# The D-skip term of a Mamba-2 scan: from a VectorE product to diagonal matmuls in the PSUM accumulation

## The reference, cut to what matters

```
h = rmsnorm(x);  proj = h @ w_in          # z_ssd, x/B/C, dt, q, k, v, z_sb, gates
xs, B, C = silu(conv4(xbc));  dt = softplus(dt_raw + dt_bias);  a = -exp(a_log)
# scan, per chunk and head:
attn   = (C B^T) * exp(segment sums of dt*a), lower triangle
y_diag = attn @ (xs * dt)
y_off  = exp(cumsum) * (C @ prev_state);  prev_state = decay * prev_state + B^T (xs*dt*decay)
y      = y_diag + y_off + xs * d_skip[head]          # the D-skip term is the last product
y      = group_rmsnorm(y * silu(z_ssd)) @ w_ssd_proj
o      = stick_breaking(q, k, v) * silu(z_sb) @ w_sb_proj
out    = x + rmsnorm((sigmoid(g1) * y_ssd + sigmoid(g2) * y_sb) @ w_out)
```

## Time and profile before

| | |
|---|---|
| runs | 1963.42 us median of 3 (1962.96 to 1964.13) |
| profiled execution | 1959.76 us; span 1958.1 us on its slowest core (core 4) |
| spans of the 8 cores | 1953.8 to 1958.1 us |
| TensorE | busy 1495.8 us (76%) |
| ScalarE | busy 1210.3 us (62%) |
| VectorE | busy 912.4 us (47%) |

### The profile page before, as it was taken

One profiled execution on the slowest core, in us unless ns is written; L12 is line 12 of the kernel. 1 busy time (PEld: TensorE's weight loads), 2 busy tenths in 40 slices (PEclk: granted clock), 3 DMA queues, 4 the chain that ended last, 5 costly groups with the idle time before them and its releaser, 6 DMA issues.

```text
span 1958.1 us, 28450 instructions; the slowest of 8 cores (1953.8 to 1958.1 us)
## 1 busy us (share of the span) xinstructions
PE 1495.8 (76%) x7452; PEld 722.4 (37%) x7452; DVE 912.4 (47%) x1822; ACT 1210.3 (62%) x2508; POOL 52.2 (3%) x58
## 2 busy tenths in 40 slices
PE   1666456666666988877988789877777789999984
PEld 1333254444443534422343234432222234444431
DVE  4455537888887553433443344433333322323344
ACT  2355414445445088999899988999999952221132
POOL 0000000000000300000000000000000010000000
PEclk9988757777777999999999999999999999999997
DMA  7710020000000111000010000110000071242056
GB/s 191 114 23 1 0 33 1 1 1 1 1 1 1 22 12 23 3 10 1 1 23 12 1 1 2 22 23 1 1 1 1 1 95 14 22 42 24 11 162 194
DMA packets 52186, 53.48 MB, mean 27 GB/s; under 512 B 19648, under 2 KB 45376, under 8 KB 52032
## 3 DMA queue, kind: packets, MB, share of 16 engines
q0 software_dynamic: 43824, 24.38, 10.8%
q1 hardware_dynamic: 8208, 27.27, 4.5%
HBM read 67.64 MB, written 8.39 MB: 39 GB/s over the span
## 4 chain that ended last, share of the span: by engine, by line
PE 44%; ACT 25%; DVE 14%; issue 12%; DMA 4%; ACTq 0%; DVEq 0%; SPq 0%; POOLq 0%
PE ps L384 15%; ACT et L824 7%; ACT wtb L854 6%; ACT spb L830 6%; PE ps L864 5%; DVE acc L455 4%; PE ps L390 4%; PE ps L583 3%; PE ps L952 3%; PE ps L957 3%; PE ps L847 3%; DMA y<-xb 3%; PE ps L817 2%; PE ps L851 2%; DVE Lmat L564 2%
## 5 line engine op out<-in xcount | busy, mean ns | idle before, releaser
L824 ACT ACTIVATE et<-ps 128x512 f32<-128x512 f32 (+3 forms) x640 | 375.5, 587 | 89.5 <-PE ps L821 63.9
L830 ACT ACTIVATE spb<-et 128x512 bf16<-128x512 f32 (+3 forms) x640 | 401.1, 627 | 1.6 <-ACT wtb L854 0.4
L384 PE MATMUL ps<-hT,wst 128*128 128x512 bf16 x1664 | 389.4, 390 | 6.2 <-issue 3.0
L838 DVE TENSOR_TENSOR Ssum<-Ssum,spb 128x512 bf16<-128x512 bf16 (+3 forms) x512 | 193.2, 377 | 415.9 <-ACT spb L830 325.9
L854 ACT ACTIVATE wtb<-ps 128x512 bf16<-128x512 f32 (+3 forms) x640 | 381.4, 596 | 2.6 <-PE ps L851 2.3
L864 PE MATMUL ps<-wtb,vtok 128*128 128x512 bf16 (+3 forms) x640 | 220.5, 344 | 155.5 <-ACT wtb L854 149.6
L384 PEld LDWEIGHTS ps<-hT,wst 128*128 128x128 bf16 x1664 | 164.9, 100 | 203.8 <-issue 28.0
L847 PE MATMUL ps<-spb,cb 128*128 128x512 bf16 (+3 forms) x640 | 220.9, 345 | 10.2 <-ACT spb L830 4.3
L817 PE MATMUL ps<-qz,kT 128*128 128x512 bf16 (+3 forms) x640 | 220.3, 346 | 0.0
L851 PE MATMUL ps<-Ssum,cb 128*128 128x512 bf16 (+3 forms) x576 | 197.1, 342 | 0.0
L864 PEld LDWEIGHTS ps<-wtb,vtok 128*128 128x128 bf16 x640 | 61.5, 96 | 337.7 <-issue 329.2
(11 more groups left out here) (111 smaller groups left out, 1613.8 us busy)
## 6 DMA issues: line engine op xcount, KB each, us to landing
xbuf<-x SPq DMA_DIRECT2D x17, 512.0 KB, 3.6
xb<-x SPq DMA_DIRECT2D x16, 512.0 KB, 4.4
y<-xb SPq DMA_DIRECT2D x16, 512.0 KB, 5.1
wst<-w_in POOLq DMA_DIRECT2D x12, 512.0 KB, 9.7
wst<-w_in POOLq DMA_DIRECT2D x5, 1024.0 KB, 12.5
wst<-w_in POOLq DMA_DIRECT2D x16, 256.0 KB, 6.2
wz<-w_in POOLq DMA_DIRECT2D x2, 1024.0 KB, 15.7
wA<-w_ssd_proj POOLq DMA_DIRECT2D x2, 1024.0 KB, 17.3
```

The costliest lines, as they stand in the source:

```text
L384: K.op("pe", lambda e, c=c: e.matmul(ps[bank][:], lhsT=wt[:, c, coff:coff + 128], rhs=hT[:, c, g * 512:(g + 1) * 512], start=(c == 0), sto ...
L824: K.op("act", lambda e: e.activation(out=e_[:, q0:512], in_=ps[bA][:, q0:512], func=AF.Exp), r=[B_ps[bA]], w=[be])
L830: K.op("act", lambda e: e.activation(out=s__[:, q0:512], in_=e_[:, q0:512], func=AF.Ln, bias=1.0, scale=1.0), r=[be], w=[bsp])
L838: K.op("dve", lambda e: e.tensor_tensor(out=Sn[:, q0p:512], in0=So[:, q0p:512], in1=s__[:, q0p:512], op=ALU.add), r=[bSo, bsp], w=[bSn])
```

## The change

The D-skip product L596 and its `yield` go. Ahead of the scan's loop VectorE builds 32 diagonal 128x128 bf16 matrices `DI`: for each head D rounded to bf16, and the remainder of D, again on a diagonal. In `front`, each of the 16 matmuls of L618 is followed by two more of the same shape, with the two diagonal matrices of its head as stationary operand and the same slice of `xs_tok` as moving operand, accumulated into the same 64 columns. The two additions of L623 become plain copies from PSUM. In the lines of the changed kernel everything behind L553 stands 14 lines further down at first, 13 after the shortened loop: L583 is L597, L609 is L618, L618 is L628 with the new L632, L623 is L637, L638 is L651, L658 is L671, L676 is L689, L688 is L701.

```diff
--- before.py
+++ after.py
@@ -553,6 +553,20 @@
     B_prev = [Buf(), Buf()]
     prevbf = sb("prevbf", [128, 1024], BF16)
     B_prevbf = [Buf(), Buf()]
+    DI = sb("DI", [128, 32, 128], BF16)
+    B_DI = Buf()
+    dsp = sb("dsp", [128, 48])
+    dspb = sb("dspb", [128, 16], BF16)
+    B_dsp = Buf()
+    K.op("dve", lambda e: e.tensor_copy(out=dspb[:], in_=hv[:, 32:48]), r=[B_par], w=[B_dsp])
+    K.op("dve", lambda e: e.tensor_copy(out=dsp[:, 0:16], in_=dspb[:]), r=[B_dsp], w=[B_dsp])
+    K.op("dve", lambda e: e.tensor_tensor(out=dsp[:, 16:32], in0=hv[:, 32:48], in1=dsp[:, 0:16], op=ALU.subtract),
+         r=[B_dsp, B_par], w=[B_dsp])
+    for h in range(16):
+        for k_ in range(2):
+            K.op("dve", lambda e, h=h, k_=k_: e.tensor_scalar(out=DI[:, 2 * h + k_, :], in0=CF(CI_ID),
+                                                               scalar1=dsp[:, 16 * k_ + h:16 * k_ + h + 1], scalar2=None, op0=ALU.mult),
+                 r=[B_dsp, B_cf], w=[B_DI])
     sst = sb("sst", [128, 8])
     B_sst = [Buf(), Buf()]
     B_sst2 = Buf()
@@ -593,11 +607,6 @@
             in1=dts[:, 6, c, :].unsqueeze(2).to_broadcast([128, 16, 64]), op=ALU.mult),
             r=[B_xs[c], B_dts], w=[bxw])
         yield
-        K.op("dve", lambda e: e.tensor_tensor(
-            out=yA_[:].rearrange("p (h d) -> p h d", h=16), in0=xs_tok[:, c, :].rearrange("p (h d) -> p h d", h=16),
-            in1=hv[:, 32:48].unsqueeze(2).to_broadcast([128, 16, 64]), op=ALU.mult),
-            r=[B_xs[c], B_par], w=byA)
-        yield
         for r_ in range(4):
             if r_ + 1 < 4:
                 seg(r_ + 1)
@@ -615,14 +624,18 @@
             for hh in range(4):
                 h = r_ * 4 + hh
                 g = h // 8
-                K.op("pe", lambda e, h=h, g=g: e.matmul(
-                    ps[5 + g][:, (h % 8) * 64:(h % 8 + 1) * 64], lhsT=attnT[:, h, :], rhs=xs_tok[:, c, h * 64:(h + 1) * 64],
-                    start=True, stop=True), r=[B_attn[h], B_xs[c]], w=[B_ps[5 + g]])
+                osl = ps[5 + g][:, (h % 8) * 64:(h % 8 + 1) * 64]
+                K.op("pe", lambda e, h=h, osl=osl: e.matmul(
+                    osl, lhsT=attnT[:, h, :], rhs=xs_tok[:, c, h * 64:(h + 1) * 64],
+                    start=True, stop=False, skip_group_check=True), r=[B_attn[h], B_xs[c]], w=[B_ps[5 + g]])
+                for k_ in range(2):
+                    K.op("pe", lambda e, h=h, osl=osl, k_=k_: e.matmul(
+                        osl, lhsT=DI[:, 2 * h + k_, :], rhs=xs_tok[:, c, h * 64:(h + 1) * 64],
+                        start=False, stop=(k_ == 1), skip_group_check=True), r=[B_DI, B_xs[c]], w=[B_ps[5 + g]])
             yield
         for g in range(2):
-            K.op("dve", lambda e, g=g: e.tensor_tensor(out=yA_[:, g * 512:(g + 1) * 512], in0=ps[5 + g][:],
-                                                       in1=yA_[:, g * 512:(g + 1) * 512], op=ALU.add),
-                 r=[B_ps[5 + g], byA[g]], w=[byA[g]])
+            K.op("dve", lambda e, g=g: e.tensor_copy(out=yA_[:, g * 512:(g + 1) * 512], in_=ps[5 + g][:]),
+                 r=[B_ps[5 + g]], w=[byA[g]])
             yield
 
     def back(c):
```

## The result

| | median, us | ratio to before (95%) |
|---|---|---|
| before | 1963.6 | |
| changed kernel | 2007.7 | 1.022 (1.0209 to 1.0232) |

The changed kernel is 44 us slower. The sum gave +31.9, the forecast 1995; the measured time is near the upper end of the range (1978 to 2011). In some executions of every kernel the cores of one die, or of both, run longer at a lower granted clock; the ratios and the spans of executions given here leave those out.

The account below looks back on a forecast made before the run. It took the chain of z projection, SiLUs, table load and Exp into `dec` to bound the loop, not VectorE. Loop 18.2 + setup 11.7 + first chunk 2 = +31.9 us on the median 1963.4 gave 1995.3; range 1978 to 2011.

Parts of the forecast that it names:

- the projection queued behind block 0: Loop, TensorE: z projection L390 now stands behind block 0, starts 2.5 us later per iteration, delaying the third group's `dec`.
- The bound: VectorE's wait for the third group's `dec` ends by projection, SiLUs, table load, Exp; removing L596's 1.13 us ahead gains nothing.
- VectorE's 83%: VectorE's busy share of the 14 full iterations; sole support for the 4% rival that VectorE paces the loop, 1947 us.
- the slack: Between the projection's end and the second SiLU: 0.8 us per iteration, taken off the projection's 2.5 us delay.
- the sum: Per iteration: +2.5 - 0.8 + 0.05 - 0.45 = +1.3 us, bounds +0.9 and +1.8; times 14, +18.2 us.
- The diagonal matmuls: TensorE, block 1 behind the projection: 12 matmuls, each with a weight load of 0.097, take 1.1 us.
- The clock credit: Transposes and L635 at iteration's end run at clock 1.00 through denser TensorE work: -0.45 us per iteration, bounds 0 and 0.8.
- The rival: TensorE's wait in block 0 makes its clock rise later, slowing the projection: +1.8 us x14, 25 us more, 2020 us; 10%.
- a projection at half speed: Listed sign of being wrong: the loop's z projection running at TensorE's lower clock; an earlier one took 5.43 against 3.62 us.
- Ahead of the loop: 35 VectorE instructions building the diagonal matrices before the first `Lmat`, 32 at 0.34 us: +11.7 us, bounds 6 and 15.
- First chunk and iteration 0: `front(0)` and iteration 0: extra weight loads in four blocks between `seg`s on TensorE cost +2 us, bounds 0 and 4.
- the sum of all upper bounds: Loop 25, setup 15, first chunk and iteration 0 4: +44 us, that is 2007 us.

Follow-up runs that it names:

- matrices built in the wait: Changed kernel with the diagonal matrices built before VectorE's wait for `exa`: 1993.7 us; with the empty yield put back too: 1969.2 us.
- the run without L596: Kernel before with L596 left out, its yield kept, additions from PSUM made copies, D-skip term missing from the result: 1962.1 us, 1.0008.
- the run with the yield: Changed kernel with one empty yield put back where L596 stood, restoring the order of the kernel before: 1982.9 us, 1.0104.
- The moved projection: Changed kernel, matrices built before the wait for `exa`, z projection moved from `back(c)` into `front(c)`: 1933.3 us, 0.9856.
- filling the gap: Changed kernel with four idle 128x256 matmuls in block 0 behind the second head, where TensorE waits for VectorE: 2000.9 us, 1.0196.
- the fastest order: z projection moved into `front(c)`, yield between L591 and L596 gone: 1933.3 us with the fold, 1936.6 with L596 instead, 1932.9 without diagonal matmuls.

## Why the prediction was right, and where its sum was short

The sign and the main mechanism, the projection queued behind block 0, held; the loop was to take about 321 us and took 331.7. The steps from the kernel before to the changed one, each between two kernels that differ in it alone: L596 away, +0.2 us (not distinguishable from 0); diagonal matmuls, with their matrices built in the wait, +7.2; matrices built ahead of the loop instead, +13.7 (1982.9 less 1969.2); order, +24.8 (2007.7 less 1982.9). These four are one path, so they give 46 us by construction, the 44 measured and the 2 by which the kernel before differed between groups. What checks them is the second price of the matrices, in the other order: +14.0 (2007.7 less 1993.7).

*The bound.* "In such a wait a VectorE instruction removed ahead of it is worth nothing" is what the run without L596 showed for the time, and VectorE's 83% was no bound. The reason given was only half right. In the iteration of the rows the SiLUs did not wait for the projection (timeline of ScalarE, kernel before):

```profile
418.16 0.63 ACT L660 ACTIVATE prevbf<-prev 128x512 bf16<-128x512 f32 x1 [1.41 <-DVE prev L658]
418.79 1.28 ACT L665 ACT_TABLE_LOAD   x1
```

Their table load stood right behind the copy L660, which waited for VectorE's second L658, and that one stood behind L596. So VectorE, and L596 with it, was a link of the chain in 10 of the 14 iterations; in the 4 with a slow projection the load waited for L390. Without L596 the load comes up to 0.9 us earlier, waits for the projection in all 14 iterations, and the next load then waits 0.55 us for `seg(2)` in all 14. The wait for `dec` grew by 7 us, not by L596's 17. That a second chain, over TensorE, stood so close behind the first that nothing was left of the gain I had not read from the rows; this part came out by luck.

*The projection behind block 0.* Start predicted at 418.5 - 409.0 = 9.5 us into the iteration; it was 9.4. VectorE's third group was predicted at 15.9; it was 16.1 (469.45 less 453.36). The missing 0.2 is a step that I had not seen: with the projection later, `seg(2)` ends after the SiLUs, and the table load ahead of Exp waits for it too, 0.35 us. From the third group to the second L688 (now L701) 5.2 us were predicted and 5.17 measured (469.45 to 474.62). One reading in the working is slightly off: half way through the pair of SiLUs is 420.62, not 420.55, which makes the slack 0.9 and the sum 0.1 smaller.

*The diagonal matmuls.* I put a block of 12 at 1.1 us, from 12 weight loads of 0.097. When its products are ready, a block takes 0.35 us (in the run with the yield it starts at 410.74, and `seg(2)` behind it at 411.09): the loads overlap, and their duration is not their spacing. Of the 5.8 us that they cost in the loop in the order of before, 3.2 come from where they stand, between projection and `seg(2)`: the table load ahead of Exp waits 0.78 us in each of 14 iterations with them, 0.55 without. Another 1.2 us are slower projections (6 over 4 us, where the run without L596 has 4); the rest is not taken apart. In the new order block 0 stands ahead of the projection and is mostly covered by the wait for VectorE.

*The clock credit, the step that failed.* I took off 0.45 us per iteration because denser work would hold TensorE's clock up to the transposes. It did not: they and L648 ran at 0.50 as before. The work was not dense up to block 3, which fits the price above: a head's three matmuls take 0.09 us and not 0.29, while VectorE delivers a head every 0.26, so TensorE stands idle between heads (windows, from block 2 on):

```profile
469.90:473.30 3.40, 2.09 (x24) 1.37 (x24) 3.40 (x10) 1.86 (x6) 0.00 (x0) 0.79 0.00 0
```

The moved projection did bring what the credit was for: there L655 took 0.38. Without the credit the sum gives +1.75; the undisturbed iteration grew by 2.0 (21.27 in the one of the rows, 23.27 now), and slow projections did the rest. I had them as a rival with 10% and 25 us. The rival was real in size per case (1.4 to 1.6 us over 3.61) and happened in 4 of 14 iterations here, 6 us; it is also the one sign of being wrong that came ("a projection at half speed"). But the kernel before has slow projections as well, without that wait ahead of them: 4 of its 14 took 4.2 to 4.5 us and one 3.8, 3 us in all. So on the cores profiled the change adds about 3 us by them, and filling the gap, which got 6.8 us back, removed more than the change had added. "TensorE: Matmul & The Clock Gate" of the Trainium skill, "Why this matters for your kernels", asks for TensorE to be kept busy without long gaps, and by that the added matmuls were to help. The trace does not bear this out for the matmuls of the change, and does for the four of the filled gap.

*Ahead of the loop.* Predicted 11.7, measured 13.1 in the trace: 0.39 per instruction and not 0.34. The gap between linked instructions was right (0.10 against 0.11); the duration was 0.286, what the trace had for 256 elements, not the 0.23 that I drew between 16 and 256. By what the Trainium skill says in "VectorE: DVE Perf Modes", "The DRAIN you can't avoid", that the semaphore costs nothing extra, there would be no gap; the trace disagrees for instructions that wait for the one before, with 3.5 us of idle time ahead of 32.

*First chunk and iteration 0.* Predicted +2, measured -0.2, where the cores of the kernel before differ by 1.3 us among themselves. That blocks are cheap, as above, would explain it; no run took it apart.

So of the 12 us by which the median missed the forecast, the loop's share is the largest: 28.8 against 18.2, of which 6.3 are the credit that was not paid and about 3 the slow projections. The loop and the setup together missed by 12.0 us, and the 2.2 that the first chunk did not cost hid a part of it. The measured 2007.7 lies just above 2007, the sum of all upper bounds; it is in the range because that was drawn "somewhat over the upper bound".

## What to carry to other kernels

Before you take work off the busiest engine, look at what ends its waits, and at what stands close behind that: here chains over TensorE and ScalarE held the loop, and 18 us of VectorE work could be deleted without effect. When the program's order comes from generators that are interleaved by `yield`, removing an instruction together with its step reorders all engines; print the order of both and look for a long instruction group that slid behind a dependency. Build constants ahead of a wait, not behind it (14 us here). Move the long independent piece (the z projection) out of the chain first, and try it in more than one order: the move alone gave 5 us in the order of before and 27 in the other, with the fold or without.

## What the runs showed of the hardware

- TensorE's granted clock rises at a time within the iteration that differs from iteration to iteration, though the work is the same: 6.0 to 8.8 us into ten iterations of the changed kernel and 12.3 to 12.7 into four, whose projections took 5.04 to 5.25 us instead of 3.61. A wait of 0.95 us or more for VectorE stands ahead of fast and slow projections alike. With four matmuls in that wait none of 14 was slow, on any core. Two more for comparison: the kernel before, without that wait, had 4 of 14 at 4.2 to 4.5 us, and the one with the yield alone taken out had 12 of 14 at 4.9 to 5.3.
- Small matmuls 128x64 with a fresh 128x128 bf16 weight load each come 0.03 us apart at the higher clock when nothing is waited for (12 in 0.35 us), though the record of a load lasts 0.1 us.
- A VectorE tensor_scalar from f32 to bf16 took 0.286 us for 128x128, as much as one from f32 to f32 for 128x256 (0.29). They differ in the output type and in the scalar, which the first reads from a tile and the second has as a constant; no run took this apart.
- A ScalarE table load of 1.28 us was not hidden in the wait of the instruction behind it: in the row at 464.73 it waited 2.04 us for the projection that the SiLU reads, and loaded only then; in all 14 iterations of the changed kernel it waited for L390.
- What stays open: what paces the fastest order. VectorE is busy there in 237.87 of 275.40 us; the diagonal matmuls do not change its time measurably, and L596's 18 us change it by about 4, in few executions.
